# Token mixing of a diffusion block in phases: attention beside the output product of two tiles back, the next norm's scalings in a phase's first steps

## The reference, cut to what matters

```python
for l in range(2):                                   # D = 1024, SwiGLU width 2816
    h = h + 0.5*g2*swiglu(norm_modulate(h, ...))      # feed-forward 1, context columns too
    n = norm_modulate(h, norm_mix, shift, scale)      # rmsnorm(h)*(1+scale)+shift
    u, q, k, v = split(n @ w_in)                      # 512, 512, 128, 128 wide
    pool = pool_mixer(u) @ w_pool * pool_scale        # centred means over 2, 4, 8, 16 tokens
    q, k = rope(q), rope(k)
    attn = softmax([window of 3 blocks of 128, 256 context keys, sink]) @ v   # 8 heads, 2 KV heads
    h = h + g5 * (concat([pool, attn]) @ w_out)       # mixing
    h = h + 0.5*g8*swiglu(norm_modulate(h, ...))      # feed-forward 2
out = rmsnorm(h, norm_final)
```

## Time and profile before

| | |
|---|---|
| time, median of 3 runs | 2917.92 us (2917.41 to 2920.98) |
| profiled execution | 2925.55 us, span of its slowest core 2924.0 us |
| busy share of the span | PE 91%, DVE 30%, ACT 27%, POOL 13% |
| chain of waits, share of the span | PE 85%, issue 4%, DVE 4%, ACT 3%, DMA 3%, POOL 1% |
| mixing of layer 0, 685.8 to 1011.4 us | 325.6 us |
| mixing of layer 1, 2150.0 to 2448.5 us | 298.5 us |

### The profile page before, as it was taken

The page is one execution under the profiler, slowest core; times in us unless marked ns, Lnnn a source line. Parts: engine busy times, 40 slices in busy tenths (PEclk is TensorE's granted clock), DMA queues, the critical chain, the costliest instruction groups (busy, mean ns, idle before and its releaser), DMA issues.

```text
span 2924.0 us, 46537 instructions; the slowest of 8 cores (2909.7 to 2924.0 us)
## 1 busy us (share of the span) xinstructions
PE 2666.2 (91%) x16692; PEld 1406.1 (48%) x16976; DVE 866.4 (30%) x1568; ACT 798.4 (27%) x1276; POOL 389.3 (13%) x572
## 2 busy tenths in 40 slices
PE   3899999997888799999899999999977888999998
PEld 1455555553444355555455555555534444444445
DVE  2211221214555511132123222222134553112224
ACT  3211321112454511132123112311125453122122
POOL 2111001002322211101100000000023221000000
PEclk9899999998999899999999999999989999999999
DMA  9466356352000165545644341344520003434453
GB/s 212 78 101 107 53 98 103 73 103 48 8 12 6 28 117 97 92 82 87 109 77 79 61 78 32 71 71 78 94 57 8 14 1 66 73 63 88 79 96 130
DMA packets 75706, 214.42 MB, mean 73 GB/s; under 512 B 9184, under 2 KB 17120, under 8 KB 74976
## 3 DMA queue, kind: packets, MB, share of 16 engines
q0 software_dynamic: 60896, 187.33, 37.8%
q1 hardware_dynamic: 14592, 24.12, 2.6%
HBM read 390.32 MB, written 8.39 MB: 136 GB/s over the span
## 4 chain that ended last, share of the span: by engine, by line
PE 85%; issue 4%; DVE 4%; ACT 3%; DMA 3%; POOL 1%; SPq 0%; DVEq 0%; ACTq 0%; POOLq 0%
PE ps L125 74%; PE ps L123 11%; DMA arena<-wab 2%; ACT arena L761 1%; DVE arena L459 1%; ACT arena L468 1%; DMA arena<-gains 1%; DVE arena L663 1%; POOL arena L418 0%; DVE arena L513 0%; SPq L143 0%; DVE arena L788 0%; DVE arena L684 0%; ACT arena L661 0%; ACT arena L429 0%
## 5 line engine op out<-in xcount | busy, mean ns | idle before, releaser
L125 PE MATMUL ps<-arena 128*128 128x512 bf16 (+8 forms) x14581 | 2511.2, 316 | 200.2 <-ACT arena L761 45.6
L125 PEld LDWEIGHTS ps<-arena 128*128 128x128 bf16 (+1 forms) x14829 | 1242.4, 98 | 1290.1 <-issue 274.1
L123 PE MATMUL ps<-arena 128*128 128x512 bf16 (+6 forms) x2111 | 657.0, 335 | 50.8 <-ACT arena L415 26.8
L565 DVE TENSOR_TENSOR arena<-arena,ps 128x512 bf16<-128x512 f32 (+2 forms) x484 | 291.9, 603 | 1184.4 <-PE ps L123 1128.9
L563 ACT ACTIVATE arena<-ps 128x512 f32<-128x512 f32 (+2 forms) x484 | 256.1, 529 | 1183.4 <-PE ps L123 1178.2
L513 DVE SCALAR_TENSOR_TENSOR arena<-ps,arena 128x512 f32<-128x512 f32 (+3 forms) x296 | 177.1, 609 | 569.5 <-PE ps L123 569.3
L123 PEld LDWEIGHTS ps<-arena 128*128 128x128 bf16 (+1 forms) x2147 | 207.2, 99 | 220.9 <-issue 85.6
L468 ACT ACTIVATE arena<-arena 128x512 bf16<-128x512 f32 (+3 forms) x256 | 179.6, 725 | 275.6 <-DVE arena L459 192.8
L143 POOL DMA_DIRECT2D arena<-wab x176 | 94.0, 538 | 645.3 <-PE ps L123 643.5
L761 ACT ACTIVATE arena<-ps 128x1024 bf16<-128x1024 f32 x167 | 161.7, 1027 | 53.3 <-PE ps L123 49.1
L459 DVE TENSOR_TENSOR arena<-arena 128x512 f32<-128x512 f32 (+3 forms) x256 | 156.2, 631 | 26.4 <-ACT arena L431 15.1
(11 more groups left out here) (34 smaller groups left out, 196.2 us busy)
## 6 DMA issues: line engine op xcount, KB each, us to landing
arena<-wab POOLq DMA_DIRECT2D x176, 512.0 KB, 6.5
arena<-wo POOLq DMA_DIRECT2D x64, 704.0 KB, 7.8
arena<-wmod POOLq DMA_DIRECT2D x144, 256.0 KB, 6.5
outT<-arena SPq DMA_DIRECT2D x26, 256.0 KB, 2.4
arena<-xT SPq DMA_DIRECT2D x8, 640.0 KB, 16.5
arena<-xT SPq DMA_DIRECT2D x16, 256.0 KB, 11.0
arena<-wout POOLq DMA_DIRECT2D x4, 1024.0 KB, 10.9
arena<-win POOLq DMA_DIRECT2D x2, 1536.0 KB, 13.1
```

What stands on the lines that cost most here:

```text
L123: self.ops["pe"].append(lambda e, l=l, r=r, o_i=o_i, st_i=st_i, sp_i=sp_i: e.matmul(o_i, l, r, start=st_i, stop=sp_i, skip_group_check=sha ...
L125: self.ops["pe"].append(lambda e, l=l, r=r, o_i=o_i, st_i=st_i, sp_i=sp_i: e.matmul(o_i, l, r, start=st_i, stop=sp_i, skip_group_check=sha ...
L565: S.op("dve", lambda e: e.tensor_tensor(gTb[:, j, off:off + n], sa_s[pi][:, 0:n], pb[pi][:, 0:n], ALU.mult), reads=[("sa", pi), BK[2 + pi] ...
```

## The change

- `mix` becomes a row of phases. Phase t (0 to 4) merges two lists by weights given to each step: on one side `wout_steps` of the group of tile t-2, then `a_steps(t)` with the pooling of tile t-1 inside it and the sums of the next norm; on the other side the attention of tile t-1. The groups are now whole tiles. A tail phase has the output product of tile 3, the pooling of tile 4 and the attention of the last group; a last phase has the output product of tile 4.
- The norm of tile t+1 (`col_norm`) has its squares on POOL in pieces of 256 columns and its sums in phase t, and its scalings among the first five output steps of phase t+1. In phase 4 and the tail phase, this is the norm for the feed-forward after the mixing.
- The norms of tiles 0 and 1 are both done in the output steps of the feed-forward before (`mix_tail`); tile 0 has its own buffer `nTt0`, in the place of `aot`.
- In `rope`, ACT alone reads the bank (a float32 copy), POOL makes the bf16 copy from it, DVE multiplies from SBUF.
- All input products, output products, pooling, sums and transposes of phases 1 to 4 and of the tail phase go round banks 6 and 7. Phase 0 has six banks.
- `aot` has two buffers, `qT` two and not three. `band` is loaded at the start of `mix`. The first two weight pieces of the next feed-forward are loaded after phase 4 (`pre_load`).
- Pooled tiles are copied by ACT, transposes by DVE, u by DVE from tile 1 on.
- At the start: the biases and gains are loaded before x; `mod_first` uses four banks in turn and not one; the squares and sums of tile 0's norm come one step earlier, its scalings are spread over three steps of tile 2.

```diff
-            groups = [[b for b in range(4 * t - 1, 4 * t + 3) if qlo <= b < qhi] for t in range(5)]
+            groups = [[b for b in range(4 * t, 4 * t + 4) if qlo <= b < qhi] for t in range(5)]
...
-                S.op("act", lambda e: e.copy(qsb[qi][:, 0:n], src[:, 0:n]), reads=[sk], writes=[("qsb", qi)])
-                S.op("dve", lambda e: e.tensor_tensor(ra[:, 0:n], src[:, 0:n], dcos, ALU.mult), reads=[sk, ("cs", 0)], writes=[ka, sk])
+                S.op("act", lambda e: e.copy(ra[:, 0:n], src[:, 0:n]), reads=[sk], writes=[ka])
+                S.op("pool", lambda e: e.tensor_copy(qsb[qi][:, 0:n], ra[:, 0:n]), reads=[ka], writes=[("qsb", qi)])
+                S.op("dve", lambda e: e.tensor_tensor(ra[:, 0:n], ra[:, 0:n], dcos, ALU.mult), reads=[ka, ("cs", 0)], writes=[ka])
...
+            def wout_steps(blks, side=()):
+                out = []
+                for d in range(8):
+                    out.append((1.8, lambda d=d: wout_step(blks, d)))
+                    out += [(0.0, f) for f in side[d * len(side) // 5:(d + 1) * len(side) // 5]]
+                return out
...
+            for t in range(5):
+                dense = wout_steps(groups[t - 2], scales) if t >= 2 else [(0.0, f) for f in scales]
+                mine = a_steps(t, pool_steps(t - 1) if t else [])
...
+                if nxt:
+                    squares, sums, scales = nxt
+                    at = len(mine) // 2
...
+                        part[0:0] = [(0.0, f) for f in sqs] if i else []
+                        mine += part + [(0.9, sums[i])]
+                    mine[2:2] = [(0.0, f) for f in squares[0]]
...
+                merge(dense + mine, attn_steps(groups[t - 1]) if t else [])
...
+            side = [(0.8, f) for f in scales] + sums_of(norms[1]) + [(0.8, f) for f in norms[1][2]]
+            merge(wout_steps(groups[3]) + pool_steps(4), attn_steps(groups[4]), side)
...
+            merge(wout_steps(groups[4]), side)
...
-            late = [(1, {0: norms[2][0], 1: norms[2][1], 2: norms[2][2], 3: norms[0][0]}),
-                    (2, {1: norms[0][1], 2: norms[0][2]}), (0, {})]
+            late = [(1, {0: norms[2][0], 1: norms[2][1], 2: norms[2][2] + norms[0][0], 3: norms[0][1]}),
+                    (2, {0: norms[0][2][0:3], 1: norms[0][2][3:6], 2: norms[0][2][6:8]}), (0, {})]
```

More of the change, by code:

```diff
@@ L338, in hkeys @@
             return [("h", k, b) for b in range(c0 // 128, (c0 + n + 127) // 128)]
+        S.dma("sp", None, bm_l[0], bmod[0], writes=[("bm", 0)])
+        S.dma("sp", None, gn_l[0], gains[0], writes=[("gn", 0)])
         x_load(512, 512)
@@ L528, in build, with pre_load @@
         pre_in = {}
+        def pre_load(l, f):
+            cnt["ab"] = 2
+            for j in range(2):
+                pre_in[l, f, j] = j
+                S.dma("pool", None, wab_s[j], wab[l, f, j].rearrange("p (a k c) -> p a k c", a=2, k=8), writes=[("wab", j)])
         def ffn(l, f, i_norm, segs, extra=(), tail=lambda nm: ([],), by_tile=None, late=()):
@@ L616, in mix_loads @@
                     lambda: S.dma("pool", None, wq, win[l, :, :, WKV:WCOLS], writes=[("wq",)]),
[L617 to L624, removed]
+                    lambda: S.dma("pool", None, cm, cmask, writes=[("cm",)])]
@@ L638, in mix @@
             S.dma("pool", None, wou, wout[l, :, 4:8, :], writes=[("wou",)])
+            S.dma("pool", None, band, bandT, writes=[("band",)])
             S.op("act", lambda e: e.activation(esb, esb, AF.Exp), reads=[("esb",)], writes=[("esb",)])
@@ L657, in proj, with evac @@
                 return ps[b], BK[b]
-            def evac(dst, src, reads, writes):
-                if busy_act[0] == 0 and take("ev", 2) == 0:
+            def evac(dst, src, reads, writes, eng=None):
+                if eng == "act" or (eng is None and take("ev", 2) == 0):
                     S.op("act", lambda e: e.copy(dst, src), reads=reads, writes=writes)
@@ L698, in a_steps @@
                 hold = {}
+                nTc, nname = (nTt, "nTt") if t else (nTt0, "nTt0")
+                nk = [(nname, k) for k in range(8)]
                 def cs_load():
@@ new lines, in wout_steps, with pool_steps @@
+            def wout_steps(blks, side=()):
+                out = []
+                for d in range(8):
+                    out.append((1.8, lambda d=d: wout_step(blks, d)))
+                    out += [(0.0, f) for f in side[d * len(side) // 5:(d + 1) * len(side) // 5]]
+                return out
+            def pool_steps(t):
+                return [(0.4, lambda g=g: pool_step(groups[t], g)) for g in range(4)]
+            i_next, (c0n, nn) = tail
+            norms = [col_norm(l, i_next, c0n + off, n,
+                              lambda k, o2, m, off=off: nTb[:, k, off + o2:off + o2 + m],
+                              lambda k, sti=sti: [("nT", k, sti)], proj) for sti, (off, n) in enumerate(subtiles(nn))]
@@ L956, in l0_first @@
         def l0_first():
-            mod_load(0)
             curp["par"] = 0
```

218 lines of the change are left out of this document (129 added, 89 removed).

## The result

The change is slower: 2949.73 us median of 4 runs (2947.64 to 2952.36) against 2917.92 in the same job (three runs, 2917.41 to 2920.98), a ratio of 1.0107 (95% interval 1.0087 to 1.0126). A fourth run of the kernel before took 3228 us: some executions of every kernel here are slower as a whole, at a lower granted clock, and they are left out of every ratio. Forecast were 2796 us. So some 30 us were lost where 122 were to be gained.

A forecast was written before the change was run, and what follows sets the result against it. PE's gaps and low clock were taken as the time to win. Mixings 53.6 and 62.5 us, plus 9 at the start, less 3.5 for the moved norm, made 121.6 off 2917.9: 2796 us, range 2755 to 2860.

The forecast's parts named there:

- So nothing, up to 2 us a phase: Rope: POOL's copy lengthens bank to permutation by 1.2 us, hidden by a 1.73 us step; cost nothing to 2 us a phase.
- the bank free 0.9 us earlier: Rope: the input product's bank is released 0.9 us sooner because DVE no longer reads it.
- Port: DVE products with two SBUF inputs and POOL reads exclude each other: 2.7 us more a phase, mostly hidden, some 15 if not.
- Full phases, 54 us: Phases 2 to 4 of layer 0: 45.3 us PE work, 1.5 for tight output steps, 7 for the rest; ends 48 and 62.
- signs of being wrong: Full phases above 60 us, PE waits for exponentials over 26 us a layer, or residuals late behind products waiting on `tmp_s`.
- Tail and last phase, 51 us: End of layer 0's mixing: tail 35 us, bound by ACT and DVE; last phase 16 us, including 3 to 5 until feed-forward.
- Program start, 9 us: Gains loaded first gain 1 us and the 11.5 us wait before tile 0 goes; 9 us in all, ends 0 and 11.
- The moved norm's 3.5 us: Tile 1's norm sums in the feed-forward's output steps: 1.7 us more in each layer, 3.5 us cost.
- Coupling of attention and scalings: Rival: scores wait through exponential, scaling, DVE product and normalisation in each full phase; phases 62, 56 us more, 2852 us; chance 0.18.
- PE-bound: Rival: PE's work alone limits the mixings; phases 48, tails 28, 50 us less, 2746 us; chance 0.12.
- The clock rival: Rival: gaps return and PE runs at 1.2 GHz in the phases; at 40% it costs 143 us, 2939 us; chance 0.08.
- My argument against: Against the clock rival: in the kernel before, a mixing round with PE gaps of about 1 us stood at clock 1.00.

The follow-up runs named there:

- experiment 5: Changed kernel with the rope of before and each permutation behind its own u step: 0.9898 of the kernel before; 2883.7 to 2888.3 us in four executions, 2907.8 and 2913.7 in two.
- Experiment 12: Changed kernel with the start of before, cosine product written to the second buffer and sine product to the first: 0.9941 of the kernel before, 2904.2 to 2905.3 us.
- Experiment 4: Changed kernel, new rope kept, with the permutation of each q behind its own u step and not behind the next q: 0.9971 of the kernel before.
- experiment 13: Changed kernel with the start of before, the two rope buffers swapped, and each permutation behind its own u step: 0.9931 of the kernel before, 2898.3 to 2906.1 us.
- experiment 1: Changed kernel with only the rope of before (ACT writes the bf16 copy, DVE multiplies from the bank): 0.9898 of the kernel before, 2889.8 and 2890.1 us.
- experiment 8: Kernel before with only the new program start: 1.0062 of the kernel before; two executions 2919.5 and 2919.6 us, the others 2940.9 to 2946.4.
- experiment 10: Changed kernel with the rope of before, each permutation behind its own u step, and the start of before: 0.9906 of the kernel before, 2887.4 to 2892.7 us.
- experiment 6: Changed kernel, new start kept, with cosine product written to the second buffer and sine product to the first: 0.9987 of the kernel before, 2895.3 to 2928 us in two heaps.
- experiment 11: Changed kernel with rope of before, permutations behind their own u steps, and squares of tail and last phase on ACT: 0.9921 of the kernel before, 2893.3 to 2897.5 us.

## Why the prediction was wrong

Where the phases of layer 0 lie is read from PE on core 3: the first matmuls of the mixing, of the output products with which phases 2 and 4 and the tail phase begin, and of the next feed-forward. Kernel after:

```profile
682.63 1.67 PE L125 MATMUL ps<-arena 128*128 128x512 bf16 x7
...
759.63 1.67 PE L125 MATMUL ps<-arena 128*128 128x512 bf16 x7 [0.94 <-DVE arena L719]
...
899.26 1.67 PE L125 MATMUL ps<-arena 128*128 128x512 bf16 x7 [0.83 <-DVE arena L719]
...
962.20 1.67 PE L125 MATMUL ps<-arena 128*128 128x512 bf16 x7 [0.87 <-DVE arena L719]
...
1027.29 1.67 PE L125 MATMUL ps<-arena 128*128 128x512 bf16 x7
```

and with the rope and order of before (experiment 5):

```profile
676.07 1.67 PE L125 MATMUL ps<-arena 128*128 128x512 bf16 x7
...
740.52 2.98 PE L125 MATMUL ps<-arena 128*128 128x512 bf16 x7 [0.94 <-DVE arena L719]
...
864.52 1.67 PE L125 MATMUL ps<-arena 128*128 128x512 bf16 x7 [0.83 <-DVE arena L719]
...
921.82 1.67 PE L125 MATMUL ps<-arena 128*128 128x512 bf16 x7 [0.83 <-DVE arena L719]
...
985.90 1.67 PE L125 MATMUL ps<-arena 128*128 128x512 bf16 x7
```

So, in us:

| | forecast | after | rope and order of before |
|---|---|---|---|
| phases 0 and 1 | 59 | 77.0 | 64.5 |
| phases 2 and 3 | 108 | 139.6 | 124.0 |
| phase 4 | 54 | 62.9 | 57.3 |
| tail and last phase | 51 | 65.1 | 64.1 |
| sum | 272 | 344.7 | 309.8 |

The kernel before takes 325.6 us between the same two marks. In layer 1 the forecast was 236; the kernel after takes 307.7, experiment 5 takes 273.0, the kernel before 298.5.

**The step that failed is "So nothing, up to 2 us a phase" for the rope.** Measured, over both layers: 34 us alone on the kernel before (ratio 1.0116), 60 us in the phases (1.0107 against 0.9898). The parts that I looked at were right: POOL's copy is even shorter than taken (0.61 us, not 1.0), and the squares stand ahead of it. What I followed was PE's path from the bank to the permutation, which the steps between cover but for 3.4 us in layer 0. What I did not ask is who else waits for the copy. The cosine product overwrites the copy's input, so DVE waits for POOL, by some 42 us more in one layer than without that write, with the sine products and the copies of u behind it, each holding one of two banks. I had named the bank free 0.9 us earlier as a gain, and that bank is; the others are held longer. Experiment 12 shows the size: other buffers, the same operations, give back 48 us (1.0107 to 0.9941). Experiment 4 shows the other half of the same wait: with the permutation behind its own u step the next q's product no longer stands before the sine product, and 40 us come back. The two cures do not add up (experiment 13 against 12: 0.1%; experiment 5 against 1: 0.2% at most), so what they save is one and the same time of PE, though only experiment 12 removes DVE's wait for the copy.

**Port.** By the Trainium skill ("SBUF — State Buffer", Who interferes with whom), a VectorE instruction with two SBUF inputs and a GpSimd one that reads SBUF exclude each other. The rows agree with the rule: 1.44 us beside a square, 1.02 beside half squares. I weighed it at 15 us at most. What remains of the new rope in experiment 12 is 10 us, for the port and the third hop together; the port alone was not tried. The 6.41 us in the tail phase I did not foresee, since I gave each product half of one POOL instruction. That product stayed through nearly the whole row, where 25 of 27 did not, and in experiment 5, with the rope of before, it takes 6.41 us too, so it is no part of the rope's cost.

**Full phases, 54 us: too low by 7 to 8 in phases 2 and 3 even without the new rope** (62 each, 57 for phase 4). PE was busy for 52.6 of 61 at clock 0.97; the waits left are many and short (exponential, both rope products, u, pooling's copies). That they come of having two banks is likely, but the number of banks was not tried. The upper end, 62, was the better number. Of the signs of being wrong that the prediction names, the first came, full phases above 60 us (70 in the kernel after); waits for exponentials of 26 us a layer did not (13.7). Phases 0 and 1 are 5.5 us above the forecast once the rope is undone.

**Tail and last phase, 51 us: they take 65 and 64** with either rope. 6 us are the product beside the squares. The rest is shown only as waits for exponentials and copies and a low clock (PE busy 45.2 of 64 us, 0.87); which of ACT, DVE and the two banks sets it was not tried.

**Program start, 9 us: measured 2.7** in the trace, 0 to 7 us in the runs (experiments 8 and 10). The wait before tile 0 shrank by 5 us. But tile 1's norm comes later: its exponential starts at 33.82 us on core 3, and at 32.80 on core 0 in experiment 8, against 29.50 in the earlier trace rows, where 1 us was allowed for the gains loaded first. That is more than the 2.2 us wait that it removes. The moved norm's 3.5 us were not tried alone.

**The rivals.** Coupling of attention and scalings did not happen where I put it: that part of phase 3 ran at clock 1.00. In the tail phase the case of the 6.41 us is a chain of that kind. PE-bound: no. The clock rival gave 2939 us, close to the result, and that is luck. It took 40% as a share of PE's work, but in round 5 it was a share of the time, and at half speed 40% of the time does a quarter of the work: that costs 90 us and not 143, and gives 2886. Its mechanism, gaps that keep returning and a clock that falls, is there in part. The clock stands at 0.86 in the part of the phase with the rope's waits and at 1.00 in the other, and over layer 0's mixing at 0.91 against 0.95 in experiment 5. An estimate from these windows: 62 us of the mixing at the lower level against 31, so up to 16 of the 35 us between the two are clock, lost because of the waits and given back with them. By the Trainium skill ("TensorE: Matmul & The Clock Gate", HAM oscillation) a PE that idles again and again between groups pays for it in clock; the trace agrees in that the part with waits of about 2 us is the one with the lower clock. My argument against, that round 2 with gaps of about 1 us stood at 1.00, did not reach to these.

**The sum.** Of the 122 us forecast, the change without its rope gives about 30 (experiments 1, 5, 10); the two mixings give 16 and 25 of the 54 and 62 that were forecast for them. The rope takes 60. That is the result, 30 us slower.

## What to carry to other kernels

When a copy moves to another engine, list every instruction that reads or writes its input and output, not only the one that needs the result. A write in place behind a read on another engine is a wait, and on an engine in program order all the unrelated work behind it waits too. It is cured by a second buffer; here one was at hand, and no operation was added.

Where few banks go round, judge an edit by how long each bank is held, through all that stands before its reader on its engine. To shorten the hold of one bank by 0.9 us is no gain if another is held for 2 us more.

Undo each part of a change that bundles several: here one part hid the gain of the other, and the best version (ratio 0.988 to 0.991) is the change without three of its lines.

## What the runs showed of the hardware that was not expected

- With the new start, on one of three chips, two or more cores (all eight in experiment 6's trace) were granted a clock of 0.81 or 0.82 from about 105 us on, with PE busy for 98% of the time, and ended about 25 us later. In experiment 8's trace core 7 has 0.81 in every 10 us from 110 to 260 us, and groups of eight matmuls follow at 2.09 us, where they follow at 1.73 at full clock: a steady value between the two levels, and not a change from one to the other. By their spans it was so in most executions of experiments 6 and 8 and in two of 5; the executions of the kernel before that they are compared with, on the same chip, all took 2916 to 2926 us. On the other two chips no execution of a kernel with this start that is compared here shows it. Why is open; the order of loads and the earlier matmuls in the first 100 us are all that differs in experiment 8.
- A VectorE product of two SBUF inputs that started inside a row of 12 GpSimd squares (7.33 us) took 6.41 us, and one in layer 1 took 5.69. The other 25 of the two mixings that overlapped squares in the same trace took at most 1.18 us, inside rows of 8 and 12 too. So such a product mostly gets its turn after the square that runs, and now and then, for a reason that is open, hardly before the row ends. With the squares on ACT (experiment 11) the long one is gone.
